# Feed-forward norm of the second block: the root taken out of the transpose and multiplied into the up projection's results

## What is computed

```python
def rms_norm(x, g, eps=NORM_EPS):
    y = xf * lax.rsqrt(jnp.mean(xf * xf, axis=-1, keepdims=True) + eps)
    return (y * g.astype(jnp.float32)).astype(x.dtype)

def conv_ffn(x, g, w_up, conv_w, conv_b, w_down):
    h = rms_norm(x, g) @ w_up                 # (256, 1024) @ (1024, 5632)
    acc = conv_b + hp[:, 0:t] * conv_w[0]     # hp: h with two empty tokens ahead
    for i in range(1, CONV_W):
        acc = acc + hp[:, i:i + t] * conv_w[i]
    gate, val = jnp.split(acc, 2, axis=-1)
    return (jax.nn.silu(gate) * val) @ w_down # (256, 2816) @ (2816, 1024)
```

## Time and profile before

| | |
|---|---|
| median of 3 runs | 1075.38 us (1075.04 to 1075.98) |
| the profiled execution | 1074.92 us, of which the span from first to last instruction is 1073.1 us |
| PE busy | 1063.8 us, 99% of the span |
| DVE busy | 781.5 us, 73% |
| ACT busy | 642.5 us, 60% |
| mean granted TensorE clock | 1.000 |
| HBM traffic | 168 GB/s over the span |

### The profile page before, as it was taken

One profiled execution on the slowest core, in us unless ns is written; L12 is line 12 of the kernel. 1 busy time (PEld: TensorE's weight loads), 2 busy tenths in 40 slices (PEclk: granted clock), 3 DMA queues, 4 the chain that ended last, 5 costly groups with the idle time before them and its releaser, 6 DMA issues.

```text
span 1073.1 us, 21320 instructions
## 1 busy us (share of the span) xinstructions
PE 1063.8 (99%) x7745; PEld 931.8 (87%) x7745; DVE 781.5 (73%) x1370; ACT 642.5 (60%) x1160; POOL 15.0 (1%) x29
## 2 busy tenths in 40 slices
PE   9999999999999999999999999999999999999998
PEld 7978888888887788888888988898999979999997
DVE  5877766667896676666687888656764968877776
ACT  5876555544676765445568974445567357666663
POOL 1000000000000000000010000000000000000000
PEclk9999999999999999999999999999999999999999
DMA  8636555555665346555564543122255645656662
GB/s 323 248 133 216 190 184 194 195 184 170 213 216 155 103 156 197 189 182 181 190 221 135 175 136 103 49 76 76 80 177 176 180 155 178 196 180 191 183 190 97
DMA packets 49170, 181.75 MB, mean 169 GB/s; under 512 B 5537, under 2 KB 5697, under 8 KB 48209
## 3 DMA queue, kind: packets, MB, share of 16 engines
q1 hardware_dynamic: 46800, 170.41, 48.8%
q0 software_dynamic: 1584, 7.63, 2.4%
q10 hardware_dynamic: 720, 2.79, 0.7%
HBM read 179.74 MB, written 1.07 MB: 168 GB/s over the span
## 4 chain that ended last, share of the span: by engine, by line
PE 86%; DVE 8%; ACT 3%; issue 1%; DMA 1%; ACTq 0%; DVEq 0%
PE acc L774 25%; PE work L717 8%; PE work L701 7%; PE work L704 7%; PE work L705 7%; PE work L720 4%; PE acc L701 4%; PE acc L705 3%; PE acc L704 3%; DVE wlo L2093 3%; ACT whi L1472 2%; PE work L722 1%; PE work L757 1%; DMA sqr<-x_t 1%; PE work L926 1%
## 5 line engine op out<-in xcount | busy, mean ns | idle before, releaser
L2093 DVE TENSOR_TENSOR wlo<-raw,whi 128x1024 fp32r<-128x1024 f32 x317 | 382.5, 1223 | 87.1 <-ACT whi L1472 85.2
L1472 ACT ACTIVATE whi<-raw 128x1024 fp32r<-128x1024 f32 x319 | 335.4, 1058 | 50.1 <-PE work L701 18.9
L701 PE MATMUL work<-xhl,whi 128*128 128x256 f32 x544 | 154.4, 284 | 0.9 <-ACT k_ L1818 0.2
L704 PE MATMUL work<-xhl,whi 128*128 128x256 f32 x544 | 152.7, 281 | 0.0
L705 PE MATMUL work<-xhl,wlo 128*128 128x256 f32 x544 | 152.7, 281 | 0.0
L717 PE MATMUL work<-xhl,whi 128*128 128x512 f32 x420 | 148.9, 393 | 0.0
L720 PE MATMUL work<-xhl,wlo 128*128 128x256 f32 x480 | 124.7, 280 | 0.0
L774 PE MATMUL acc<-whi,hh 128*128 128x512 f32 x344 | 109.6, 396 | 0.7 <-DVE hl L2108 0.7
L774 PE MATMUL acc<-whi,hl 128*128 128x512 f32 x344 | 109.0, 395 | 0.0
L774 PE MATMUL acc<-wlo,hh 128*128 128x512 f32 x344 | 108.9, 395 | 0.0
L701 PEld LDWEIGHTS work<-xhl,whi 128*128 128x128 f32 x544 | 102.5, 188 | 5.4 <-DVE sm L2272 1.6
(11 more groups left out here) (464 smaller groups left out, 1900.5 us busy)
## 6 DMA issues: line engine op xcount, KB each, us to landing
raw<-weights SPq DMA_DIRECT2D x319, 512.0 KB, 3.7
gb<-ln_rows POOLq DMA_DIRECT2D x4, 1024.0 KB, 6.7
memraw<-mem_t SPq DMA_DIRECT2D x1, 1024.0 KB, 7.2
x<-mem_tok SPq DMA_DIRECT2D x1, 1024.0 KB, 5.8
x<-x_tok ACTq DMA_DIRECT2D x1, 1024.0 KB, 6.6
qlat<-bias_scratch POOLq DMA_DIRECT2D x1, 1024.0 KB, 11.1
qlat<-bias_scratch POOLq DMA_DIRECT2D x4, 256.0 KB, 4.3
out_tok<-res SPq DMA_DIRECT2D x4, 256.0 KB, 2.1
```

The source lines that it names most:

```text
L701: a = mm(dst, whi[:, n % RING, col], hi, start=start, stop=False, skip_group_check=shared)
L704: mm(dst, whi[:, n % RING, col], lo, start=False, stop=False, skip_group_check=shared)
L1472: act_fn(whi[:, n % RING, :], raw[:, n % RING, :], ACT.Copy).then_inc(cut_hi, 1)
L2093: tt(wlo[:, n % RING, :], raw[:, n % RING, :], whi[:, n % RING, :].bitcast(F32), ALU.subtract).then_inc(cut_lo, 1)
```

## The change

`feature_major_unscaled` transposes x itself, each bank as soon as x is added up, with no zero products ahead. ACT squares two pieces of x before the gain copies and two after them, behind the cut of `out`'s last slot; the root comes after that. The two scalings of x on DVE and ACT go away. PE spreads the root over 128 partitions with two small matmuls after `chunk_pair`, ACT copies the result to `roots`. In the feed-forward stage DVE writes `cg` and `cv` as result x `roots` (`ffn_scale`), where ACT copied them before; ACT takes its first tap from `cg` and `cv`, after DVE has written them. The wait for the banks is now ended by `ffn_scale`; PE's down product waits for a signal `ffn_cut`, ACT's sigmoid for `gate_taps`.

```diff
@@ PE
+            def feature_major_unscaled(name, made):
+                open_result((name, 0))
+                for d, t in ((0, 0), (0, 1), (1, 0), (1, 1)):
+                    for i in ((4, 3) if (d, t) == (1, 0) else ((0, 1, 2), (3, 4))[d]):
+                        if t == 0 and i < 4:
+                            pe.wait_ge(sig("x_made"), made + i + 1)
+                        for c, dst in turned_chunks(name, i):
+                            last = nc.tensor.transpose(dst[:, half(t)], x[:, t, c * P:c * P + P], C("ident"))
...
-            feature_major("rms2", 13)
+            feature_major_unscaled("rms2", 4)
...
             chunk_pair("ffn", [("ffn", 0), ("ffn", 1)], "rms2")
+            bank = open_result(("ffnroot", 0))
+            pe.wait_ge(sig("rstd"), NORMS["rms2"] + 1)
+            for t in range(2):
+                last = mm(bank[:, half(t)], column("rstd", t).broadcast_to([P, P]), C("ident"), start=True, stop=True)
+            close_result(last, ("ffnroot", 0))
 
             def ffn_down(f, n, it=None):
-                wait_drained(pe, ("ffn", 2 * f + 1), it, 8)
+                pe.wait_ge(sig("ffn_cut"), f + 1 if it is None else it * 4 + (f + 1))
@@ ACT
-            rms_norm("rms2", "norm2", 4)
+            for q in range(2):
+                square_piece(x, "x_made", 4, q)
+            gained_high("rms2", "norm2")
             cuts("out", DC - 1)
-            act.wait_ge(sig("cg_zero"), 2)
+            for q in range(2, 4):
+                square_piece(x, "x_made", 4, q)
+            act.wait_ge(sig("rinv"), NORMS["rms2"] + 1)
+            act_fn(norm_column("rstd"), norm_column("var"), ACT.Sqrt).then_inc(sig("rstd"), 1)
...
             def ffn_gate(f, it=None):
 
-                bank = wait_filled(act, ("ffn", 2 * f), it, 8)
-                act_fn(cg[:, f % 2, 2:T + 2], bank[:, 0:T], ACT.Copy).then_inc(sig("gate_in"), 1)
-                first_tap(fa[:, f % 2, :], bank, f, it, False).then_inc(sig("gate_in"), 1)
+                wait_drained(act, ("ffn", 2 * f), it, 8)
+                first_tap(fa[:, f % 2, :], cg[:, f % 2, 2:T + 2], f, it, False).then_inc(sig("gate_in"), 1)
 
             def ffn_value(f, it=None):
 
-                bank = wait_filled(act, ("ffn", 2 * f + 1), it, 8)
-                act_fn(cv[:, f % 2, 2:T + 2], bank[:, 0:T], ACT.Copy).then_inc(sig("value_in"), 1)
-                first_tap(fb[:, f % 2, :], bank, f, it, True).then_inc(sig("value_in"), 1)
-                wait_drained(act, ("ffn", 2 * f), it, 8)
+                wait_drained(act, ("ffn", 2 * f + 1), it, 8)
+                first_tap(fb[:, f % 2, :], cv[:, f % 2, 2:T + 2], f, it, True).then_inc(sig("value_in"), 1)
+                act.wait_ge(sig("gate_taps"), f + 1 if it is None else it * 4 + (f + 1))
                 act_fn(fs[:, f % 2, :], fa[:, f % 2, :], ACT.Sigmoid).then_inc(sig("sigm"), 1)
...
             for f in range(2):
                 cuts("ffn", 2 * f)
+                if f == 0:
+                    bank = wait_filled(act, ("ffnroot", 0))
+                    drain(act_fn(roots, bank[:, 0:T], ACT.Copy), ("ffnroot", 0))
                 ffn_gate(f)
@@ DVE
-            rms_norm("rms2", "norm2")
+            gained_low("rms2", "norm2")
             cuts("out", DC - 1)
+            inverse("rms2", False)
...
+            def ffn_scale(dst, k, it=None):
+                bank = wait_filled(dve, ("ffn", k), it, 8)
+                drain(tt(dst[:, k // 2 % 2, 2:T + 2], bank[:, 0:T], roots, ALU.mult), ("ffn", k))
+
             def ffn_gate(f, it=None):
                 p = f % 2
-                dve.wait_ge(sig("gate_in"), upto(2 * f + 2, it, 8))
-                drain(conv(fa[:, p, :], cg[:, p, :], it, f, False), ("ffn", 2 * f))
+                dve.wait_ge(sig("gate_in"), upto(f + 1, it, 4))
+                conv(fa[:, p, :], cg[:, p, :], it, f, False).then_inc(sig("gate_taps"), 1)
...
             for f in range(2):
                 cuts("ffn", 2 * f)
+                if f == 0:
+                    wait_drained(dve, ("ffnroot", 0))
+                ffn_scale(cg, 2 * f)
+                ffn_scale(cv, 2 * f + 1)
                 ffn_gate(f)
+                cuts("ffn", 2 * f + 1)
                 ffn_value(f)
-                cuts("ffn", 2 * f + 1)
                 ffn_low(f)
 
             def ffn_step(f, it=None):
                 cuts("ffn", 3 * f + 4, it, 12)
+                ffn_scale(cg, 2 * f + 4, it)
+                cuts("ffn", 3 * f + 5, it, 12)
                 ffn_gate(f + 2, it)
-                cuts("ffn", 3 * f + 5, it, 12)
+                ffn_scale(cv, 2 * f + 5, it)
+                cuts("ffn", 3 * f + 6, it, 12)
                 ffn_value(f + 2, it)
-                cuts("ffn", 3 * f + 6, it, 12)
                 ffn_low(f + 2, it)
```

More of the change, by code:

```diff
@@ L291 @@
 _results("rms2", [0])
-_results("ffn", range(2 * FC2))
+_results("ffn", range(2))
+_results("ffnroot", [0])
+_results("ffn", range(2, 2 * FC2))
 RESULT = {key: n for n, key in enumerate(RESULTS)}
@@ L444, in column @@
             return norm_column(name, 4)[:, 2 * d + t:2 * d + t + 1]
+        roots = stat[:, 2, :]
         def turned_chunks(name, i):
@@ L799, in feature_major @@
                             last = nc.tensor.transpose(dst[:, half(t)], rest[:, t, c * P:c * P + P], C("ident"))
+                        if t == 1 and i < 4:
+                            last.then_inc(sig("turned"), 1)
+                        elif t == 1:
+                            close_result(last, (name, 0))
+            def feature_major_unscaled(name, made):
[6 more added lines that the diff above has]
+                            last = nc.tensor.transpose(dst[:, half(t)], x[:, t, c * P:c * P + P], C("ident"))
                         if t == 1 and i < 4:
@@ L1527, in _, with square_piece @@
             table(ACT.Sqrt, of_tokens("large", 1))
+            def square_piece(src, ready, done, q):
+                t, d = divmod(q, 2)
+                act.wait_ge(sig(ready), done + q + 1)
+                act_fn(tok(sqrt_, t, d), tok(src, t, d), ACT.Square, scale=D ** -0.5, accum_out=column("square", t, d))\
+                    .then_inc(sig("squared"), 1)
             def square_pieces(name, src, ready, done, ahead=None, logarithm=False):
@@ L1532, in square_pieces @@
                 for q in range(4):
[L1533 to L1536, removed]
+                    square_piece(src, ready, done, q)
                 if ahead:
@@ L1575, in rms_norm, with gained_high @@
                     ahead()
+                gained_high(name, g)
+            def gained_high(name, g):
                 for i in range(5):
@@ L2027, in _, with first_tap @@
                 cuts("out", j)
-            rms_norm("rms2", "norm2", 4)
+            for q in range(2):
+                square_piece(x, "x_made", 4, q)
+            gained_high("rms2", "norm2")
             cuts("out", DC - 1)
-            act.wait_ge(sig("cg_zero"), 2)
-            def first_tap(dst, bank, f, it, is_value):
+            for q in range(2, 4):
+                square_piece(x, "x_made", 4, q)
+            act.wait_ge(sig("rinv"), NORMS["rms2"] + 1)
+            act_fn(norm_column("rstd"), norm_column("var"), ACT.Sqrt).then_inc(sig("rstd"), 1)
+            def first_tap(dst, src, f, it, is_value):
                 col = f + (FC2 if is_value else 0)
@@ L2038, in first_tap @@
                                 par[:, bass.ds(it * 4 + (PCOL[name] + col), 1)] for name in ("conv2", "conv_b")]
-                return act_fn(dst, bank[:, 0:T], ACT.Identity, scale=scale, bias=shift)
+                return act_fn(dst, src, ACT.Identity, scale=scale, bias=shift)
             def ffn_gate(f, it=None):
-                bank = wait_filled(act, ("ffn", 2 * f), it, 8)
-                act_fn(cg[:, f % 2, 2:T + 2], bank[:, 0:T], ACT.Copy).then_inc(sig("gate_in"), 1)
-                first_tap(fa[:, f % 2, :], bank, f, it, False).then_inc(sig("gate_in"), 1)
+                wait_drained(act, ("ffn", 2 * f), it, 8)
+                first_tap(fa[:, f % 2, :], cg[:, f % 2, 2:T + 2], f, it, False).then_inc(sig("gate_in"), 1)
             def ffn_value(f, it=None):
-                bank = wait_filled(act, ("ffn", 2 * f + 1), it, 8)
-                act_fn(cv[:, f % 2, 2:T + 2], bank[:, 0:T], ACT.Copy).then_inc(sig("value_in"), 1)
-                first_tap(fb[:, f % 2, :], bank, f, it, True).then_inc(sig("value_in"), 1)
-                wait_drained(act, ("ffn", 2 * f), it, 8)
+                wait_drained(act, ("ffn", 2 * f + 1), it, 8)
+                first_tap(fb[:, f % 2, :], cv[:, f % 2, 2:T + 2], f, it, True).then_inc(sig("value_in"), 1)
+                act.wait_ge(sig("gate_taps"), f + 1 if it is None else it * 4 + (f + 1))
                 act_fn(fs[:, f % 2, :], fa[:, f % 2, :], ACT.Sigmoid).then_inc(sig("sigm"), 1)
@@ L2173, in rms_norm, with gained_low @@
                     ahead()
+                gained_low(name, g)
+            def gained_low(name, g):
                 for i in range(5):
@@ L2753, in upto @@
```

(19 more changed lines are left out.)

## The result

The changed kernel takes 1164.45 us (median of 4 runs, 1164.13 to 1164.78) against 1075.22 before: a ratio of 1.083, interval 1.0818 to 1.0843. The forecast was 1161.5, in a range of 1147 to 1180. The profiled execution is of 1164.15 us.

The account below looks back on a forecast made before the run. A ring of waits between ACT and DVE, not PE, was to bound the kernel: 906.3 after two groups, 16 steps of 12.66, three of 12.06, last group 11.1, ending at 1156.2 (+86.3); forecast 1161.5 us, range 1147 to 1180.

Parts of the forecast that it names:

- The ring: Feed-forward loop: ACT and DVE wait for each other in list order, nothing overlaps, PE outside it; chance 0.86.
- 12.66 us a step: Looped feed-forward steps: sum of the DVE and ACT waits once around, against 8.49 us of PE work.
- 12.06 in the steps written straight out: Three unlooped steps: value part 1.50 instead of 1.78, and 0.32 saved by two hops and the gate taps.
- The hop from DVE's scaling to ACT's tap: Loop: delay between DVE's scaling and ACT's tap, taken as 0.15 us within bounds 0.03 to 0.15.
- One sign: Loop: PE's busy share was to be near 0.67, with PE idling some 4.2 us a step.
- The head: Norm before the loop: transposes end 2.7 us earlier, root costs under 0.5, 1.6 us left at slot 4.
- group 0: First feed-forward group, ahead of the loop: 9.73 us, from 887.5 to 897.2, including a table load.
- Slot 4: Cut in group 0 at 892.8 where PE asks at 892.2; before, it was asked for at 894.4.
- rounds of the loop: Hardware loop: listed among unknown costs, each round may add some 0.2 us.
- the last down product: End of the last group: PE's start and last down product together 3.17 us.
- The rival that came true in one place: Loop: PE's clock falls as PE idles, time between 1161 and 1250 us; chance 0.08.
- The rival of the other side: Loop: DVE's added work fits in PE's 8.49 us step, time 1073.2 to 1073.8, 1072.5 at best; chance 0.05.

Follow-up runs that it names:

- run 1: Changed kernel with ACT's loop list alone reordered, each cut ahead of the tap behind which it stood; 1078.90 us, ratio 1.0039.
- run 5: Changed kernel with one swap in ACT's loop list, cut B ahead of the gate tap; 1127.61 us, ratio 1.0483.
- run 6: Changed kernel with DVE's loop list alone altered, the value part ahead of the low part of C; 1120.00 us, ratio 1.0416.
- run 2: Changed kernel with each scaling product on DVE done twice, first into a tile nobody reads; 1178.43 us, ratio 1.0962.
- run 3: Changed norm with the loop of the kernel before, the root left out of the up products' results; 1073.21 us, ratio 0.9985.
- run 4: Changed loop with the norm of the kernel before, so the root is applied twice; 1166.12 us, ratio 1.0848.
- Run 7: Changed kernel with 15 zero products on PE in its last wait, ahead of the last down product; 1162.77 us, ratio 1.0815.
- run 8: Changed kernel with every ACT cut ahead of the tap, in loop and first two groups, DVE's lists there to match; 1072.55 us, ratio 0.9977.

## Why the prediction was right

**The ring.** The mechanism was the one forecast: DVE waits 1.76, 2.07 and 0.52 us for ACT's cuts, where 1.6 to 2.2 and about 0.5 were named. The forecast of 12.66 us a step was measured at 12.63 in the shortest steps and 12.74 on average, that of 12.06 in the steps written straight out at 12.14 (low parts of B at 1124.21 and 1136.35). That 12.66 and 12.63 lie so near each other is partly luck, as errors of the terms cancel: the value taps and the product up to `hb` take 1.61 us (978.09 to 979.70) instead of 1.78, while both hops of the scaling, `hb` to `hh`, the low parts and the taps are 0.01 to 0.06 longer each. The hop from DVE's scaling to ACT's tap, which no row before showed, was 0.18 us (970.54 to 970.72; taken 0.15, bounds 0.03 to 0.15, so just outside them); the tap from SBUF goes on after 0.50 (taken 0.48) and the sigmoid after 0.31 (taken 0.33). Runs 1, 5, 6 and 2 open, shorten and lengthen the ring, with the results that the sum gives. One sign came out otherwise: PE's busy share of the loop is 0.73, not near 0.67. The forecast divided 8.49 by 12.66 and left out what every restart adds, so PE idles 3.4 us a step and not 4.2. That changes nothing in the time, since PE isn't in the ring. That the order of ACT's list is the cause, and not DVE's load, is shown by run 1.

**The head.** The chain was forecast to reach the first scaling of the ring at 906.3; it was 906.21. Here too errors cancel: the first scaling comes at 887.14 instead of 887.5, and group 0 takes 9.91 us instead of 9.73 (887.14 to 897.05). Slot 4 begins at 892.78 in the changed kernel (forecast 892.8, before 894.4). In run 3 it begins at 892.34, and the time is 1.7 us lower. In the changed kernel the head's gain is in the sum as an earlier start of the ring, and run 4, without the head, is 1.7 us slower.

**The sum's error.** It came out 3.0 us short (span +89.3 against +86.3), by two terms. The 19 steps to the last scaling of `cg` took 240.24 us (906.21 to 1146.45) instead of 238.8. The 16 looped steps took 203.82 of them (906.21 to 1110.03), 1.7 us more than 16 times 12.63. I had named rounds of the loop, at 0.2 each, and left them out of the sum. The excess is 0.4 a round on average; it comes back every four steps and is gone in the steps written straight out, so I put it to the rounds, though no run takes the loop away. The second term is the last down product: with PE's start I gave it 3.17 us, and from the end of `hl` (1154.52) to the last matmul's end it took 4.67. One slip of the last addition is smaller: 1161.2 and 0.46 are 1161.7, not 1161.5.

**The rival that came true in one place.** PE's clock did fall, not in the loop but at the end: PE waits 4.86 us for `hl` of the last group, and the granted clock is 0.50 between 1156 and 1158 us (the stretches above), 1.2 GHz instead of 2.4. Run 7 shows that the idle time before it is the reason: with PE busy in that wait the clock stays at full and 1.5 us of this product come back. I had worked out the wait's end but not asked what a wait of nearly 5 us does to the clock. In the loop of the changed kernel's profiled execution, with waits of PE up to 1.97 us, the clock column stays at 1.00, and the matmuls of 512 columns come every 0.235 us there, as before. By the Trainium skill's rule (TensorE: Matmul & The Clock Gate, The HAM clock gate) that idling puts the clock back to half, the end of this trace agrees.

**The rival of the other side.** "The vector work fits beside PE" was right in its arithmetic, as runs 1 and 8 show (DVE busy 132 of 152 us, PE 152 of 152), and wrong for the lists as the change has them. Its price of 1073.2 to 1073.8, 1072.5 at the best, holds for run 3 (1073.21) and run 8 (1072.55).

## What to carry to other kernels

Where engines execute fixed lists, count a step of the loop around its waits and not by busy time: an operation moved from one engine to the engine that waits for its results (here ACT's copy, moved to DVE ahead of ACT's tap) turns two parallel lists into one ring if each list has, between the two ends of the new wait, work for which the other engine waits. Work that waits for nothing new (here the cuts of the next weights) belongs ahead of the instruction with the new wait; with that the same operations cost nothing, and 92 us lay between the two orders. That they then fit is a separate question, answered by the busiest engine's own step without waits for the other's cuts (8.0 us here against PE's 8.49), not by its busy share. If a wait of several us stays ahead of a short burst of matmuls at the end, ask what clock they will run at.

## What the runs showed of the hardware that I had not expected

In the run with the scaling done twice PE's clock fell eleven times between 906 and 1150 us, though none of its waits there was longer than the changed kernel's longest (1.93 us against 1.97). One such place, PE's timeline and the clock of the stretches:

```profile
930.03 0.73 PE L778 MATMUL acc<-whi,hh 128*128 128x512 f32 x2 [1.87 <-DVE wlo L2127]
930.60 0.92 PE L778 MATMUL acc<-wlo,hh 128*128 128x512 f32 x2
```

```profile
930.00:935.00 5.00, 4.91 (x14) 3.62 (x15) 3.72 (x8) 1.36 (x2) 0.00 (x0) 0.66 0.29 105
935.00:940.00 5.00, 4.43 (x38) 4.23 (x36) 3.08 (x6) 1.55 (x2) 0.00 (x0) 1.00 0.46 122
```

The matmuls behind the wait come at 0.43 us instead of 0.235 for a few us, then at full pace again. Over 906 to 1150 us that run's mean granted clock was 0.92, and still its time rose only by what the ring gives: PE, with 8.49 us of work at full clock in a ring of 13.3, had room for it.

Which wait brings a fall and which doesn't is not settled by these runs. Runs 4 and 7 have the changed kernel's loop, and each shows three falls in it, one in every 51 us, which is a round of the hardware loop. The changed kernel's profiled execution has the same waits at the same places and no fall. Here are PE's wait and the stretch behind it, first in the changed kernel and then in run 7:

```profile
957.54 0.38 PE L705 MATMUL work<-xhl,whi 128*128 128x256 f32 x1 [1.79 <-DVE wlo L2127]
958.00:962.00 4.00, 3.70 (x32) 3.49 (x31) 2.20 (x4) 1.55 (x2) 0.00 (x0) 1.00 0.45 131
```

```profile
957.75 0.39 PE L705 MATMUL work<-xhl,whi 128*128 128x256 f32 x1 [1.80 <-DVE wlo L2129]
958.00:962.00 4.00, 4.00 (x23) 4.00 (x23) 2.02 (x4) 1.55 (x2) 0.00 (x0) 0.57 0.36 131
```

Runs 5 and 6, whose PE is busier, had two falls each in the loop. So neither the longest wait nor the busy share alone decides, and the same instructions can run with and without a fall. Of the changed kernel's four executions two have a mean clock of 0.993 over the span instead of 0.998, and are 0.6 us longer (1164.8 against 1164.1). The fall at the end varies too: behind a wait of 4.87 us run 4's last down product took 5.49 us (1156.99 to 1162.48), where the changed kernel's took 4.61.
